# A transformer block stack in split fp32: a first norm applied to results, weights' low parts in pieces, tiles moved in SBUF

## What is computed

```python
h = rms_norm(x, norm_mix)                       # x * rsqrt(mean(x*x) + EPS) * g
proj = einsum('bsd,dc->bsc', h, w_in)
u_pool, u_lru, q, k, v, g_logits = split(proj)
gates = sigmoid(g_logits + b_gate)
y_pool = pool_mixer(u_pool, w_pool, pool_scale) # (windowed mean - u) @ w_pool, * pool_scale
y_lru = rglru_mixer(u_lru, ...)                 # causal convolution of 4, two gates, linear scan
y_sb = stick_breaking_attention(rms_norm(q, q_norm), rms_norm(k, k_norm), v)
merged = sum(gates[:, :, b] * (y_b @ w_branch[b]) for b in range(3))
x = x + merged @ w_out
x = x + (silu(h2 @ w_ffn_gate) * (h2 @ w_ffn_up)) @ w_ffn_down     # h2 = rms_norm(x, norm_ffn)
```

## Time and profile before

| | |
|---|---|
| median of 3 runs | 2343.05 us (2337.33 to 2345.93) |
| the profiled execution | 2347.11 us, span 2344.4 us, mean granted clock of PE 0.988 |
| PE busy | 2258.4 us, 96% of the span |
| PE's weight loads | 1816.1 us, 77% |
| DVE, ACT, POOL busy | 951.5 us (41%), 836.8 us (36%), 933.6 us (40%) |
| weight products on PE, x as operand | L299 678.6 us, L300 674.8 us, L301 674.8 us (1728 each) |
| POOL's subtractions L824 | 895.6 us, 194 of 4617 ns |
| ACT's copies L934 | 366.8 us, 192 of 1911 ns |

### The profile page before, as it was taken

The page is one execution under the profiler, slowest core; times in us unless marked ns, Lnnn a source line. Parts: engine busy times, 40 slices in busy tenths (PEclk is TensorE's granted clock), DMA queues, the critical chain, the costliest instruction groups (busy, mean ns, idle before and its releaser), DMA issues.

```text
span 2344.4 us, 27313 instructions
## 1 busy us (share of the span) xinstructions
PE 2258.4 (96%) x10130; PEld 1816.1 (77%) x10130; DVE 951.5 (41%) x1261; ACT 836.8 (36%) x1101; POOL 933.6 (40%) x264
## 2 busy tenths in 40 slices
PE   6999999899999999999988999999998999999997
PEld 4777877788878888888866778888886777888885
DVE  5244366634461111341156643233424546332334
ACT  4326465323232222331154333332323534333321
POOL 3331233443434344554421334436544123444453
PEclk9999999999999999999999999999998999999998
DMA  3221122222222322232321222222332112222232
GB/s 145 89 90 54 54 73 90 90 97 101 90 90 89 107 89 80 98 109 90 108 63 28 72 87 92 90 90 86 110 117 85 32 53 83 97 100 89 80 99 73
DMA packets 32701, 202.80 MB, mean 87 GB/s; under 512 B 3900, under 2 KB 4156, under 8 KB 13692
## 3 DMA queue, kind: packets, MB, share of 16 engines
q1 hardware_dynamic: 29932, 192.94, 23.8%
q0 software_dynamic: 2704, 8.97, 1.4%
HBM read 199.74 MB, written 2.15 MB: 86 GB/s over the span
## 4 chain that ended last, share of the span: by engine, by line
issue 53%; PE 30%; POOL 13%; DVE 1%; DMA 1%; ACT 0%; POOLq 0%; DVEq 0%; SPq 0%; ACTq 0%; PEldq 0%
POOL w_low L824 13%; PE bank L299 8%; PE bank L301 8%; PE bank L300 8%; PE bank L496 2%; PE bank L473 2%; PE bank L483 1%; DMA raw<-wmain 0%; PE bank L469 0%; PE bank L468 0%; POOLq L214 0%; DVE qk L1290 0%; DMA distance_table<-table 0%; PE bank L778 0%; PE bank L325 0%
## 5 line engine op out<-in xcount | busy, mean ns | idle before, releaser
L824 POOL TENSOR_TENSOR w_low<-raw,w_high 128x2048 fp32r<-128x2048 f32 x194 | 895.6, 4617 | 1249.3 <-ACT w_high L934 1236.9
L299 PE MATMUL bank<-x_low,w_high 128*128 128x512 f32 x1728 | 678.6, 393 | 17.2 <-DVE x_low L1283 9.2
L301 PE MATMUL bank<-x_high,w_low 128*128 128x512 f32 x1728 | 674.8, 391 | 0.0
L300 PE MATMUL bank<-x_high,w_high 128*128 128x512 f32 x1728 | 674.8, 390 | 0.0
L934 ACT ACTIVATE w_high<-raw 128x2048 fp32r<-128x2048 f32 x192 | 366.8, 1911 | 536.9 <-PE bank L301 532.8
L299 PEld LDWEIGHTS bank<-x_low,w_high 128*128 128x128 f32 x1728 | 325.5, 188 | 91.0 <-issue 20.0
L300 PEld LDWEIGHTS bank<-x_high,w_high 128*128 128x128 f32 x1728 | 325.7, 188 | 68.5 <-issue 1.2
L301 PEld LDWEIGHTS bank<-x_high,w_low 128*128 128x128 f32 x1728 | 325.5, 188 | 68.0
L299 PE MATMUL bank<-act_low,w_high 128*128 128x512 f32 x528 | 209.0, 396 | 1.3 <-POOL w_low L824 1.3
L301 PE MATMUL bank<-act_high,w_low 128*128 128x512 f32 x528 | 208.7, 395 | 0.0
L300 PE MATMUL bank<-act_high,w_high 128*128 128x512 f32 x528 | 208.6, 395 | 0.0
(11 more groups left out here) (239 smaller groups left out, 2458.8 us busy)
## 6 DMA issues: line engine op xcount, KB each, us to landing
raw<-wmain SPq DMA_DIRECT2D x146, 1024.0 KB, 4.8
raw<-wdown SPq DMA_DIRECT2D x48, 704.0 KB, 4.1
bias<-distance_table POOLq DMA_DIRECT2D x28, 256.0 KB, 3.4
x_residual<-x SPq DMA_DIRECT2D x2, 1024.0 KB, 6.1
out<-qk SPq DMA_DIRECT2D x8, 256.0 KB, 2.0
matrices<-mats SPq DMA_DIRECT2D x1, 512.0 KB, 9.9
r_blocks<-rg POOLq DMA_DIRECT2D x1, 512.0 KB, 6.4
i_blocks<-rg POOLq DMA_DIRECT2D x1, 512.0 KB, 7.0
```

The costliest lines, as they stand in the source:

```text
L299: pe.matmul(target, sh, ml, start=start and k == 0, stop=False)
L300: pe.matmul(target, sh, mh, start=False, stop=False)
L301: last = pe.matmul(target, sl, mh, start=False, stop=stop and k == n - 1)
L824: pool.tensor_tensor(wl[:, c, :], raw[:, c, :], wh[:, c, :].bitcast(F32), ALU.subtract).then_inc(low_ready, 1)
```

## The change

**The start.** SP loads half of the first chunk, cols, x in four pieces with the chunk's second half between them, the second chunk in halves, then mats and the table's inputs. ACT makes x_high = x * norm_mix at once from x, DVE the low part, with no factor of the norm in them; the squares of x are made between these. norm_sum(0) stands behind PE's third column.

```diff
+            sp_.dma_start(raw[:, 0, first], wmain[0, :, first]).then_inc(begin_landed[0], 16)
+            sp_.dma_start(cols[:, :], cols_in).then_inc(cols_landed, 16)
+            load_x(0)
+            load_x(1)
+            sp_.dma_start(raw[:, 0, second], wmain[0, :, second]).then_inc(raw_landed[0], 16)
+            load_x(2)
+            load_x(3)
+            sp_.dma_start(raw[:, 1, first], wmain[1, :, first]).then_inc(begin_landed[1], 16)
+            sp_.dma_start(raw[:, 1, second], wmain[1, :, second]).then_inc(raw_landed[1], 16)
+            sp_.dma_start(mats[:, :, :], mats_in).then_inc(mats_landed, 16)
...
+            for k in range(KT):
+                if k % 2 == 0:
+                    piece(0, 0, k // 2)
+                pe.wait_ge(sem("xl_ready"), k + 1)
+                for j in range(2):
+                    last = products(bank[j][:, :], weights(0, j)[k:k + 1], mixed[k:k + 1], start=k == 0,
+                                    stop=k == KT - 1)
+                    if k == KT - 1:
+                        last.then_inc(sem("qk_ready"), 1)
...
+                    if t >= 6:
+                        pe.wait_ge(sem("qk_read"), t - 5)
+                    products(bank[QK_BANK[t % 6]][:, :], weights(n % 2, j), mixed, arrive=None if j else (0, n, 2))\
+                        .then_inc(sem("qk_ready"), 1)
+                    if t == 2:
+                        pe.wait_ge(mats_landed, 16)
+                        norm_sum(0)
+                    if t >= 6:
+                        qk_sum(t - 6)
```

```diff
+            begin(0)
+            act.wait_ge(cols_landed, 16)
+            split(0, 1, 2, 3)
+            squares(0)
+            finish(0)
+            split(4, 5)
+            squares(1, 2)
+            split(6, 7)
+            begin(1)
+            squares(3, 4)
+            finish(1)
+            squares(5, 6, 7)
...
             for t in range(16):
-                act.wait_ge(sem("qk_ready"), t + 1)
+                if t % 2:
+                    act.wait_ge(sem("qk_ready"), t + 1)
+                    refill(t // 2 % 2, BASE["qk"] + t // 2 + 2)
+                act.wait_ge(sem("qk_read"), t + 1)
                 if t >= 2:
                     act.wait_ge(sem("square_low"), t - 1)
-                act.activation(sq[:, t % 2, :], bank[t % 4][:, :], ACT.Square).then_inc(sem("qk_square"), 1)
-                act.activation(qk[:, t, :], bank[t % 4][:, :], ACT.Copy).then_inc(sem("qk_read"), 1)
-                if t % 2:
-                    refill(t // 2 % 2, BASE["qk"] + t // 2 + 2)
+                act.activation(sq[:, t % 2, :], qk[:, t, :], ACT.Square).then_inc(sem("qk_square"), 1)
...
 
-                x = xc[:, t % 2, :]
+                x, u = xc[:, t % 2, :], lu[t % 2][:, :]
+                dve.wait_ge(sem("tile"), TILE["lru", t])
+                dve.tensor_tensor(u, bank[t % 2][:, :], rstd[:, :], ALU.mult).then_inc(sem("lru_scaled"), 1)
+                dve.wait_ge(sem("lru_scaled"), t + 1)
+                if t >= 2:
+                    dve.wait_ge(sem("lru_ix"), t - 1)
+                dve.tensor_scalar(x, u, col("conv_w", 24 + t), col("conv_b", t), ALU.mult, ALU.add)\
+                   .then_inc(sem("lru_base"), 1)
                 dve.wait_ge(sem("lru_base"), t + 1)
                 for k in (1, 2, 3):
-                    dve.scalar_tensor_tensor(x[:, k:S], bank[t % 2][:, 0:S - k], col("conv_w", 8 * (3 - k) + t),
+                    dve.scalar_tensor_tensor(x[:, k:S], u[:, 0:S - k], col("conv_w", 8 * (3 - k) + t),
                                              x[:, k:S], ALU.mult, ALU.add).then_inc(sem("lru_conv"), 1)
...
                 w = WINDOWS[g]
+                dve.wait_ge(sem("tile"), TILE["pool", t])
+                dve.tensor_tensor(pu[:, b, 16:16 + S], bank[t % 4][:, :], rstd[:, :], ALU.mult)\
+                   .then_inc(sem("pool_read"), 1)
                 dve.wait_ge(sem("pool_read"), t + 1)
                 src, dst, shift = pu[:, b, :], pa[:, 0, :], 1
...
+                if kind[2:] == "x":
+                    for j in range(2):
+                        dve.wait_ge(sem("tile"), TILE[kind, 2 * m + j])
+                        dve.tensor_tensor((gs if m % 2 else tmpa)[:, j, :], bank[4 + j][:, :], rstd[:, :], ALU.mult)\
+                           .then_inc(sem("x_read"), 1)
                     continue
                 if kind == "wp":
```

```diff
-            def products(target, stationary, moving, start=True, stop=True):
+            def products(target, stationary, moving, start=True, stop=True, arrive=None):
 
                 n = len(stationary)
                 for k, ((sh, sl), (mh, ml)) in enumerate(zip(stationary, moving)):
+                    if arrive and k % arrive[2] == 0:
+                        piece(arrive[0], arrive[1], k // arrive[2])
                     pe.matmul(target, sh, ml, start=start and k == 0, stop=False)
                     pe.matmul(target, sh, mh, start=False, stop=False)
...
+            def piece(i, n, p):
+
+                pe.wait_ge(low_ready, i * PIECES + (PIECES * n + p + 1))
...
-            def low(i, n, c):
+            def low(i, n, c, width=S):
 
                 pool.wait_ge(high_ready, i + (n + 1))
-                pool.tensor_tensor(wl[:, c, :], raw[:, c, :], wh[:, c, :].bitcast(F32),
-                                   ALU.subtract).then_inc(low_ready, 1)
+                for p in range(PIECES):
+                    part = slice(p * width, min((p + 1) * width, CHUNK if width == S else DOWN))
+                    pool.tensor_tensor(wl[:, c, part], raw[:, c, part], wh[:, c, part].bitcast(F32),
+                                       ALU.subtract).then_inc(low_ready, 1)
```

```diff
-MIX += [("g0x", 0), ("wp", 0), ("wp", 1), ("g0x", 1), ("g0y", 0), ("g0x", 2), ("g0y", 1), ("g0x", 3), ("g0y", 2),
+MIX += [("g0x", 0), ("wp", 0), ("g0x", 1), ("wp", 1), ("g0y", 0), ("g0x", 2), ("g0y", 1), ("g0x", 3), ("g0y", 2),
...
                 if n < 16:
                     continue
-                if kind == "wp":
-                    for t in range(4 * m, 4 * m + 4):
+                if kind != "wp":
+                    mix_refill(n)
+                for t in range(4 * m, 4 * m + 4):
+                    if kind == "wp":
                         act.wait_ge(sem("tile"), TILE["wp", t | 1])
-                        act.activation(yh[:, t, :], bank[t % 4][:, :], ACT.Copy, scale=col("pool_scale", t))                           .then_inc(sem("wpool_high"), 1)
-                elif kind[2] == "x":
-                    b = int(kind[1])
-                    if 4 * b + m >= 2:
-                        act.wait_ge(sem("prod_ready"), 2 * (4 * b + m - 2) + 2)
-                    for j in range(2):
-                        act.wait_ge(sem("tile"), TILE[kind, 2 * m + j])
-                        act.activation((gs if m % 2 else tmpa)[:, j, :], bank[4 + j][:, :], ACT.Sigmoid,
-                                       bias=col("b_gate", 8 * b + 2 * m + j)).then_inc(sem("gate_ready"), 1)
-                mix_refill(n)
+                        if t == 4 * m + 2:
+                            mix_refill(n)
+                        act.activation(yh[:, t, :], bank[t % 4][:, :], ACT.Copy, scale=col("pool_scale", t))\
+                           .then_inc(sem("wpool_high"), 1)
+                for j in range(2):
+                    if kind[2:] == "x":
+                        b = int(kind[1])
+                        act.wait_ge(sem("x_read"), 8 * b + 2 * m + j + 1)
+                        g = (gs if m % 2 else tmpa)[:, j, :]
+                        act.activation(g, g, ACT.Sigmoid, bias=col("b_gate", 8 * b + 2 * m + j))\
+                           .then_inc(sem("gate_ready"), 1)
                 for t in (2 * m, 2 * m + 1):
                     if kind == "g0y":
                         act.wait_ge(sem("lru_h"), KT)
```

```diff
-    arena = top[0]
+    arena = top[0] + (base - top[0]) % 2048
```

More of the change, by code:

```diff
@@ L38 @@
 MASK_ROW = 20
+PIECES = 4
 ROWS = 21
@@ L538, in _ @@
+            for n in range(1, 8):
                 for j in range(2):
                     t = 2 * n + j
[L540 to L548 removed]
@@ L631, in column @@
                 n = MIX.index((kind, t // 2))
-                chunk(0, BASE["mix"] + n)
                 for k in range(KT):
+                    if t % 2 == 0 and k % 2 == 0:
+                        piece(0, BASE["mix"] + n, k // 2)
                     if x_ready:
@@ L1157, in _ @@
                 pair = (2 * m, 2 * m + 1)
-                for t in pair:
-                    lru_base(t)
                 mix_refill(MIX.index(("lru", m)))
```

274 lines of the change are left out of this document (133 added, 141 removed).

## The result

The changed kernel takes 2317.86 us (median of 4 runs, 2317.77 to 2321.68) against 2342.38 before: ratio 0.9901, 95% interval 0.9880 to 0.9922. The prediction was 2316 with a range of 2303 to 2334. The profiled execution has a span of 2320.0 us, 24.4 less than before.

A forecast was written before the change was run, and what follows sets the result against it. PE, busy 96% of the span, bounds the kernel; time lies in its stops, lower clock and matmul spacing. Terms summed to -26.7 us, the profiled 2347.1 to 2320.4, the median to 2316; range 2303 to 2334 (forecast's own 2307 to 2324).

The forecast's parts named there:

- The start: Kernel start: PE's first weight product near 8.95 us instead of 24.06, -15.1 us.
- What is late next: Third chunk in qk: its refill stands behind the first rescaled squares and PE stops, +3.6 us.
- The norm's other places: In v: token scales in the first stage +0.9 us, q/k factor one step later +0.6 us.
- RG-LRU: Before the gates: more DVE operations, alternating with POOL's pieces, make PE wait, +10.6 us.
- Pooled products: After pool: refill ahead of the sigmoids, but DVE's chain longer by eight rescalings, -0.6 us.
- Pieces: Low parts in pieces: ffn and down waits -9.0, x_low's entry -1.8, lower clock behind the last ffn wait -1.7 us.
- The arena: Products with act and y moving: arena's new remainder modulo 2048 saves 6.6 ns on each of 2592, -17.1 us.
- The six banks: In qk: costed at nothing, since PE may run five tiles ahead of the rescaling.
- Rival A: Arena: a tile's place is no cause of the slower spacing, 2333 us; chance 0.22.
- Rival B: PE's waits: even a met wait costs PE; at 0.1 us each +58, 2374 us, slower; chance 0.06.
- Rival C: RG-LRU: POOL's pieces miss DVE's products, that term at its lower end, 2306 us; chance 0.12.
- rival D: Start gives less: first product at 12, third chunk 6 late, 2321 us (2325 with pool's upper end); chance 0.05.

The follow-up runs named there:

- e8: Changed kernel with third chunk's refill ahead of the root, later q/k refills and v's token scales earlier, lambda's small vectors behind the q/k factor: 2306.05 us.
- e6: Changed kernel, but the RG-LRU convolution's three shifted products read the PSUM bank instead of lru_u (norm's factor left out there): 2308.69 us.
- e7: Changed kernel with ACT's refill in each RG-LRU pair behind the pair's convolution instead of ahead of it: 2309.20 us.
- e5: Kernel before with only two parts of the change, the arena's move and the low parts in pieces: 2303.43 us.
- e3: Changed kernel without the arena's move (arena where it was, 384 bytes off): 2334.09 us.
- e2: Kernel before with only POOL's low parts in pieces, PE's waits per piece and the narrower refills: 2322.74 us.
- e1: Kernel before with only the arena's start moved: 2324.97 us.
- e10: Kernel before with pieces and moved arena, but the arena 512 bytes above the weights' remainder modulo 2048: 2303.32 us.
- e11: Kernel before with pieces and moved arena, but the arena 64 bytes above the weights' remainder modulo 2048: 2311.39 us.
- e12: Kernel before with pieces and moved arena, all tiles 384 bytes higher so no distance between tiles changes: 2303.14 us.

## Why the prediction was right, and where its steps were not

The time came within 2 us, in part by luck, because errors cancelled. Split at the entry to ffn0, the forecast's terms have the changed kernel 1.2 us ahead there (with 624 of the 2592 products of the arena's term in front of it) and 25.5 gained behind it. The traces have it 6.9 late there and 31.3 gained behind it. Point by point:

- **The start**, -15.1: measured -14.2. x's first piece landed later than 1.23 us per 512 KB gives.
- **What is late next**, +3.6: the stop is 3.4 beyond the spacing, in the place named. The lower clock behind it, 1.7, I had only in the lump of +2.0.
- **The norm's other places**, +1.5: this step failed. v grew by 9.0, of which about 1.8 are four sums of squares that moved there from qk. I costed the token scales on PE (0.9, as it came) and not the queue in which their copy stands on DVE, behind 18 small operations, four of them held by POOL's pieces. The late pieces at v's first chunk were missed in the same way: DVE, and so the squares and the refills behind them on ACT, run some three columns behind PE, because qk_sum is six behind (read from the orders and timelines, not tested apart). e8 got 6.9 of qk and 6.3 of v back by positions alone.
- **RG-LRU**, +10.6: the list shows 10.4 us of waits, and the mechanism is shown by e6 and e7. The stretch grew by 13.8, and by 15.0 against e5, where the arena lies as in the changed kernel. The difference to the waits is the lower clock, in two stretches of 3.4 us behind the second and third stop (3.3 us lost), which I had not counted here, and PE's restart behind each stop.
- **Pooled products**, -0.6: the stops are 0.8 and 5.8 against 8.7. The lower clock lasts 6.8 us against 10.2, but PE stood still in the first part of both, so it costs 1.7 against 2.0. Together some 2.5 better, and the stage is 2.3 shorter in e3, where the arena lies as before. I had let the whole chain wait for DVE; most of it had slack. e2 gained 3.7 here with the pieces alone, so the new order and the rescalings did not add to the gain.
- **Pieces**, -12.5 with x_low and the clock: as sized where I had looked (13.0 in e2), and 8 more in e2 elsewhere. The term was taken from PE's waits for low parts alone. The pieces also shorten what DVE and ACT wait for, which shows in ov. Behind the entry to ffn0, e3 differs from the kernel before in the pieces alone, and it is 17.4 shorter there.
- **The arena**, -17.1: 18.6 alone, 16.2 when taken out of the changed kernel. The count of 2592 left out 192 products with the RG-LRU's lru_high and lru_low, which lie in the arena too and went from 233.2 to 226.7 ns. The two softplus products were the right sign: both their operands lay in the arena, at a distance free of the 384 bytes. (These 384 come from columns, 472 x 4 = 1888 bytes rounded up to 1920, and from small.)
- **The six banks**, 0: PE's list has no wait for a bank in qk.
- **The rule quoted for the spacing**: the Trainium skill (TensorE: Matmul & The Clock Gate, section Back-to-back issue gap) gives N / 2.4 + 2.5 for an isolated product. For a stream of weight loads and products, which this kernel is, it gives about 131 ns at 512 columns. The traces agree with neither figure, and they decide: 226.7 at the best place of the arena.
- **Rival A** is out by e1 and e3. **Rival B** is out: a window of 130 us in ffn0 (740 to 870) holds 575 products before and after, with four times the waits met in it. **Rival C** is out by the stops at the gates, **rival D** by the first product at 9.87 and a stop of 3.4.

So in the first block qk and v cost 13.7 us where I had 6.0, and the RG-LRU 3 to 4 more than I had; the pooled products gave 2 of that back. Behind it, the pieces gave 17.4 where I had 12.5.

## What to carry to other kernels

Where PE is at 96%, first look at the spacing of its products by operand: a step of 3% between tiles of the same shape was worth 18.6 us here for one line, about as much as all the waits for low parts. When an early start is bought with work moved to results, write down for every moved step the queue it joins and who stands behind it: this start won 14.6 us and lost 31.1, of which reordering alone gave 29.7 back. And expect little from one stop taken away while the next step behind it is as late as before: taking away one stop that cost 5 us gave 1.5, taking away nearly all of them together 27.

## What the runs showed of the hardware

- The distance between the two operands of an fp32r product in SBUF sets its spacing: 226.7 ns at 0 or 512 bytes off a multiple of 2048, 228.9 at 64 off, 233.0 to 233.3 at 384 off (e1, e2, e3, e10, e11, e12). e12 shows that a shift of both changes nothing.
- DVE and POOL alternate by the instruction where DVE reads two SBUF operands: 2.32 us for three products alone or with one operand in PSUM, 4.09 beside POOL, and POOL's four pieces 6.07 instead of 5.05. This holds for the smallest of operations too: of six of 128x8 two were held, and the six take 3.28 instead of 1.17. An operation with one SBUF tile was held as well (e6, 1.22 instead of 0.55).
- Waits that are met cost PE nothing that shows in 575 products.
